# Attention on Trainium2: context exponentials before local ones, and the next tile's context scores before the last tile's values

## What is computed

```python
def context_attention(q, k, v):
    s = jnp.einsum('bqhd,bkhd->bhqk', q, k).astype(jnp.float32) * (HEAD_DIM ** -0.5)
    p = jax.nn.softmax(s, axis=-1).astype(v.dtype)
    return jnp.einsum('bhqk,bkhd->bqhd', p, v)
...
    s_loc = jnp.where(mask[None, None, :, None, :, :], s_loc, -jnp.inf)
    s_ctx = jnp.einsum('brnqhd,bphd->brnhqp', qb, k_ctx).astype(jnp.float32) * scale
    p = jax.nn.softmax(jnp.concatenate([s_loc, s_ctx], axis=-1), axis=-1).astype(v.dtype)
    o = (jnp.einsum('brnhql,brnlhd->brnqhd', p[..., :L], vg)
         + jnp.einsum('brnhqp,bphd->brnqhd', p[..., L:], v_ctx))
```

## Time and profile before

| | us |
|---|---|
| median of 3 runs | 2802.64 |
| lowest and highest | 2798.75, 2804.14 |
| the profiled execution | 2806.26 |
| its span, first to last instruction | 2804.5 |
| TensorE busy | 2680.5 (96%) |
| VectorE busy | 1698.7 (61%) |
| ScalarE busy | 1258.5 (45%) |

### The profile page before, as it was taken

How to read it: one execution, slowest core, us unless ns; L and a number is a source line. 1 busy time by engine, 2 the same in 40 slices (tenths; PEclk the granted TensorE clock), 3 DMA queues, 4 the chain that set the end, 5 groups by cost and what they waited for, 6 DMA issues and landing times.

```text
span 2804.5 us, 49219 instructions
## 1 busy us (share of the span) xinstructions
PE 2680.5 (96%) x21611; PEld 2008.6 (72%) x21611; DVE 1698.7 (61%) x2007; ACT 1258.5 (45%) x1795; POOL 192.3 (7%) x180
## 2 busy tenths in 40 slices
PE   6999999999999999959999999999999999999994
PEld 3555577666666698747877787778777877887783
DVE  3699234666323244466776767676766766676664
ACT  4000134555212132245656565555655555555554
POOL 0000001110000000010110111011101100110000
PEclk9999999999999999969999999999999999999997
DMA  8222222000333372267987988798888988898884
GB/s 258 90 90 75 60 56 50 14 1 24 90 90 90 90 218 106 98 213 249 290 281 267 298 278 282 264 299 279 280 279 285 294 265 282 281 297 262 283 278 167
DMA packets 457503, 543.73 MB, mean 194 GB/s; under 512 B 26304, under 2 KB 409387, under 8 KB 457290
## 3 DMA queue, kind: packets, MB, share of 16 engines
q1 hardware_dynamic: 449610, 519.60, 56.8%
q0 software_dynamic: 7680, 20.98, 3.4%
HBM read 513.27 MB, written 27.28 MB: 193 GB/s over the span
## 4 chain that ended last, share of the span: by engine, by line
PE 89%; DVE 5%; ACT 2%; SPq 2%; DMA 2%; issue 1%; POOL 0%; DVEq 0%; POOLq 0%; ACTq 0%
PE bank L651 84%; PE bank L654 5%; DVE arena L1643 2%; SPq L387 1%; ACT arena L1267 1%; DVE arena L1716 1%; ACT arena L1265 1%; DMA arena<-in_w_attn_o 0%; DVE arena L2044 0%; DVE arena L1726 0%; DMA arena<-in_w_in 0%; DMA arena<-in_cache_ctx_v 0%; DMA arena<-xhat,arena 0%; DVE arena L1723 0%; DMA yacc<-arena 0%
## 5 line engine op out<-in xcount | busy, mean ns | idle before, releaser
L651 PE MATMUL bank<-arena 128*64 128x128 f32 (+8 forms) x3716 | 735.6, 408 | 24.9 <-ACT arena L1267 10.6
L1974 DVE TENSOR_TENSOR slot_lo<-slot,e_hi 128x2048 fp32r<-128x2048 f32 x256 | 579.3, 2289 | 166.2 <-ACT e_hi L1456 162.5
L651 PEld LDWEIGHTS bank<-arena 128*128 128x128 f32 (+3 forms) x3716 | 431.9, 165 | 293.0 <-issue 216.8
L1456 ACT ACTIVATE e_hi<-slot 128x2048 fp32r<-128x2048 f32 x256 | 481.5, 1917 | 0.0
L651 PE MATMUL bank<-e_hi,xe_hi 128*128 128x512 f32 x1024 | 418.1, 408 | 0.0
L651 PE MATMUL bank<-e_hi,xe_lo 128*128 128x512 f32 x1024 | 404.7, 395 | 0.0
L651 PE MATMUL bank<-slot_lo,xe_hi 128*128 128x512 f32 x1024 | 400.3, 391 | 0.0
L651 PE MATMUL bank<-slot,arena 128*32 128x128 f32 (+1 forms) x10240 | 363.6, 297 | 6.1 <-DVE arena L1984 3.5
L651 PEld LDWEIGHTS bank<-slot,arena 128*32 128x32 f32 x10240 | 285.2, 111 | 72.6 <-issue 34.1
L1978 DVE TENSOR_TENSOR slot_lo<-slot,e_hi 128x2048 fp32r<-128x2048 f32 x128 | 288.8, 2288 | 77.9 <-ACT e_hi L1458 77.9
L654 PE MATMUL bank<-arena 128*128 128x128 f32 (+3 forms) x1415 | 207.0, 280 | 52.3 <-DVE arena L1572 12.8
(11 more groups left out here) (221 smaller groups left out, 2540.0 us busy)
## 6 DMA issues: line engine op xcount, KB each, us to landing
slot<-in_w_gate_e SPq DMA_DIRECT2D x128, 1024.0 KB, 5.7
slot<-in_w_up_e SPq DMA_DIRECT2D x128, 1024.0 KB, 9.1
slot<-in_w_down_e SPq DMA_DIRECT2D x128, 1024.0 KB, 6.9
arena<-in_w_in SPq DMA_DIRECT2D x68, 512.0 KB, 5.2
arena<-in_w_ada SPq DMA_DIRECT2D x48, 512.0 KB, 5.0
arena<-in_w_conv_pw SPq DMA_DIRECT2D x24, 256.0 KB, 5.7
arena<-in_w_attn_o SPq DMA_DIRECT2D x24, 256.0 KB, 5.4
yacc<-arena SPq DMA_DIRECT2D x10, 512.0 KB, 2.6
```

Source lines behind the costliest of these rows:

```text
L651: return nc.tensor.matmul(out, lhsT, rhs, start=start, stop=stop)
L1456: A_(halves(e_hi[c % 2])[:, :, rows4, :], halves(slot[q])[:, :, rows4, :], ACT.Copy).then_inc(ehi_ok, 1)
L1974: V_.tensor_tensor(halves(slot_lo[q])[:, :, rows4, :], halves(slot[q])[:, :, rows4, :], halves(e_hi[c % 2])[:, :, rows4, :].bitcast(F32), ...
```

## The change

- The exponentials of a tile stand as context A, context B, local A, local B. The semaphore `p_ok` is split: `pc_ok` counts context exponentials and `pl_ok` local ones.
- The groups of transposes stand as CA, CB, LA, LB, R in place of LA, CA, LB, CB, R. VectorE copies CA, LA and LB, ScalarE copies CB and R. CA and CB wait for `pc_ok`, the others for `pl_ok`.
- TensorE's round has `scores_context(g+1)`, which waits for `pc_ok`, ahead of `weigh(g-1)`.
- `weigh` takes the context parts first.
- The load of `vc` is issued ahead of the store of `state_v`.
- The load of the mask raises `bias_in`, and the mask's own semaphore goes.

VectorE's and GpSimd's work and order stay as they are, but for GpSimd's waits.

```diff
@@ -256,7 +256,7 @@
         w_d = A["w_down_e"][0].rearrange("e (k p) n -> e p k n", p=P)
 
 
-        rows_in, dwr_in, wr_in, mask_in = (sem(n) for n in ("rows_in", "dwr_in", "wr_in", "mask_in"))
+        rows_in, dwr_in, wr_in = (sem(n) for n in ("rows_in", "dwr_in", "wr_in"))
         x_in = [sem(f"x_in{tc}") for tc in range(3)]
         kraw_in, vc_in, fg_in = (sem(n) for n in ("kraw_in", "vc_in", "fg_in"))
         wo_in = [sem(f"wo_in{q}") for q in range(KD // 2)]
@@ -282,7 +282,7 @@
             sem(n) for n in ("ln_sum", "ln_mid", "ln_sq", "ln_var", "ln_std", "ln_norm", "ln_done"))
         bias_ok = sem("bias_ok")
         s_rem, s_loc, s_ctx, s_added = sem("s_rem"), sem("s_loc"), sem("s_ctx"), sem("s_added")
-        c_max, nmax_ok, p_ok = sem("c_max"), sem("nmax_ok"), sem("p_ok")
+        c_max, nmax_ok, pc_ok, pl_ok = sem("c_max"), sem("nmax_ok"), sem("pc_ok"), sem("pl_ok")
         tg_ready, tg_act, tg_dve, o_done = sem("tg_ready"), sem("tg_act"), sem("tg_dve"), sem("o_done")
         m_ready, m_sig, m_done = sem("m_ready"), sem("m_sig"), sem("m_done")
 
@@ -326,7 +326,7 @@
             nr = TILES[g % NTL][2]
             if nr == 0:
                 return [("P", True), ("R", False)]
-            return [("LA", True), ("CA", False), ("LB", True), ("CB", True), ("R", False)]
+            return [("CA", True), ("CB", False), ("LA", True), ("LB", True), ("R", False)]
 
         GROUPS = [(g, kind, by_dve) for g in range(NP) for kind, by_dve in groups(g)]
         GROUP_AT = {(g, kind): i for i, (g, kind, _) in enumerate(GROUPS)}
@@ -419,7 +419,7 @@
 
             sp.wait_ge(dw_ok, 1)
             sp.wait_ge(colv_ok, 1)
-            sp.dma_start(mask, A["window_masks"]).then_inc(mask_in, 16)
+            sp.dma_start(mask, A["window_masks"]).then_inc(bias_in, 16)
 
             def load_bias(hp):
 
@@ -439,8 +439,8 @@
             sp.wait_ge(ks_done, 2)
             sp.dma_start(O["state_k"][0, 0].rearrange("(t p) h d -> p t (h d)", p=P), kst).then_inc(state_out, 16)
             sp.wait_ge(v_done, 20)
+            sp.dma_start(vc, A["cache_ctx_v"][0, 0].rearrange("(t p) h d -> p t (h d)", p=P)).then_inc(vc_in, 16)
             sp.dma_start(O["state_v"][0, 0].rearrange("(t p) h d -> p t (h d)", p=P), vtok[:, 8:10, :]).then_inc(y_out, 16)
-            sp.dma_start(vc, A["cache_ctx_v"][0, 0].rearrange("(t p) h d -> p t (h d)", p=P)).then_inc(vc_in, 16)
             for hp in range(1, 4):
                 sp.wait_ge(b14_ok, 2 * hp)
                 load_bias(hp)
@@ -556,7 +556,6 @@
             nc.gpsimd.memset(glu, 0.0).then_inc(pads, 1)
 
             pool.wait_ge(conv_done, 1)
-            pool.wait_ge(mask_in, 16)
             def bias_rows(hp, h):
 
                 m = mask[:, 0:1, :].to_broadcast((P, SLOTS, GRID_W))
@@ -572,14 +571,16 @@
                     nc.gpsimd.tensor_tensor(b9[:, 1:9, :], b14[:, 2:10, :], mask[:, 1:9, :], ALU.add).then_inc(bias_ok, 1)
                     nc.gpsimd.tensor_tensor(b9[:, 0:1, :], b14[:, 10:11, :], mask[:, 9:10, :], ALU.add).then_inc(bias_ok, 1)
 
-            pool.wait_ge(bias_in, 64)
+            pool.wait_ge(bias_in, 64 + 16)
             for h in range(2):
                 bias_rows(0, h)
             for h in range(2):
                 bias_nine(0, h)
             for g in range(NP):
                 hp, i = divmod(g, NTL)
-                pool.wait_ge(p_ok, 2 * g + 2)
+                pool.wait_ge(pc_ok, 2 * g + 2)
+                if LOC[g]:
+                    pool.wait_ge(pl_ok, 2 * LOC0[g] + 2)
                 if g >= 2:
                     group_done(pool, g - 2, "R")
                 if LOC[g]:
@@ -590,7 +591,7 @@
                 nc.gpsimd.tensor_copy(rinv[:, g % 2, :].rearrange("p (a n) -> p a n", a=2),
                                       recip[:, g % 2, :].unsqueeze(2).to_broadcast((P, 2, DH))).then_inc(rinv_ok, 1)
                 if hp + 1 < HP and i == 1:
-                    pool.wait_ge(bias_in, 64 * hp + 128)
+                    pool.wait_ge(bias_in, 64 * hp + 128 + 16)
                     if hp == 0:
                         pool.wait_ge(ln_norm, 12)
                     else:
@@ -787,7 +788,7 @@
                 hp = g // NTL
                 qt, tok, nr, _ = TILES[g % NTL]
                 if g:
-                    pe.wait_ge(p_ok, 2 * g)
+                    pe.wait_ge(pc_ok, 2 * g)
                 for h in range(2):
                     keys = kcT[HALF[h], hp, :] if nr else kT[HALF[h], hp, TS:T]
                     last = mm(bank[3 + h][:, 0:PAST if nr else TP], qT[HALF[h], hp, P * qt:P * qt + P], keys, True, True)
@@ -798,7 +799,10 @@
                 nr = TILES[g % NTL][2]
                 for kind, _ in groups(g):
                     h = 1 if kind[1:] == "B" or kind == "P" else 0
-                    pe.wait_ge(p_ok, 2 * g + (2 if kind in ("R", "P") else h + 1))
+                    if kind in ("CA", "CB", "P"):
+                        pe.wait_ge(pc_ok, 2 * g + h + 1)
+                    else:
+                        pe.wait_ge(pl_ok, 2 * LOC0[g] + h + 1 if kind != "R" else 2 * LOC0[g + 1])
                     ring_free(pe, (g, kind))
                     out = ring_bank((g, kind))
                     if kind == "P":
@@ -827,7 +831,7 @@
                 ring_free(pe, (g, "O"))
                 out = ring_bank((g, "O"))
                 if nr:
-                    parts = [(b, vtok, tok // P + b) for b in range(4)] + [(4 + b, vc, b) for b in range(4)]
+                    parts = [(4 + b, vc, b) for b in range(4)] + [(b, vtok, tok // P + b) for b in range(4)]
                     if nr == 9:
                         parts.append((8, vtok, tok // P + 4))
                 else:
@@ -875,10 +879,10 @@
                     turn_weights(g - 1)
                 if g + 1 < NP and LOC[g + 1]:
                     scores_local(g + 1)
+                if g + 1 < NP:
+                    scores_context(g + 1)
                 if g:
                     weigh(g - 1)
-                if g + 1 < NP:
-                    scores_context(g + 1)
 
 
             pe.wait_ge(o_done, NP)
@@ -1261,10 +1265,12 @@
                 nr = TILES[g % NTL][2]
                 for h in range(2):
                     m = nmx[:, g % 2, h:h + 1]
-                    if nr:
-                        A_(Ploc[g % 2][h][:, 0:64 * nr], Ploc[g % 2][h][:, 0:64 * nr], ACT.Exp, bias=m, accum_out=sums[:, g % 2, h, 0:1])
                     n = PAST if nr else TP
-                    A_(Pctx[g % 2][h][:, 0:n], bank[3 + h][:, 0:n], ACT.Exp, bias=m, accum_out=sums[:, g % 2, h, 1:2]).then_inc(p_ok, 1)
+                    A_(Pctx[g % 2][h][:, 0:n], bank[3 + h][:, 0:n], ACT.Exp, bias=m, accum_out=sums[:, g % 2, h, 1:2]).then_inc(pc_ok, 1)
+                if nr:
+                    for h in range(2):
+                        m = nmx[:, g % 2, h:h + 1]
+                        A_(Ploc[g % 2][h][:, 0:64 * nr], Ploc[g % 2][h][:, 0:64 * nr], ACT.Exp, bias=m, accum_out=sums[:, g % 2, h, 0:1]).then_inc(pl_ok, 1)
 
             def leave_ring(g, kind):
 
```

## The result

The changed kernel takes 2810.93 us (median of 6 runs, 2809.98 to 2815.51), beside 2801.32 us for the kernel before in the same comparison (6 runs, 2798.75 to 2804.14): a ratio of 1.003, with a 95% interval of 1.0019 to 1.0041. It is slower, by about 9.6 us, and 2810.6 was predicted. The profiled execution took 2809.98 us, with a span of 2808.2.

The account below looks back on a forecast made before the run. TensorE was taken to bound rounds 3 to 6, with waits for exponentials at head pairs' ends. The terms 8.3 - 1.7 + 2.4 - 0.4 - 0.6 = +8.0 us, set on the median 2802.64, gave 2810.6 us, range 2803 to 2817.

Parts of the forecast that it names:

- boundary: First round of a head pair in the attention: 6.95 us against 7.96, 6.57 and 8.01, if at full clock.
- The loop: Attention rounds: weighing now stands in a loop through three engines, 6.95 us with 8 rows, 7.17 with 9.
- Rounds 2 to 10 and the first ones: Attention rounds: +2.1 us three times and +2.0 for the last head pair, together +8.3; first rounds -1.7.
- The -0.6: Wait for the last context exponentials at the attention's end: 3.06 us in the new order against 3.65.
- The clock: Half-clock stretches from TensorE idling in rounds 7 and 10: two of 1.2 us, +2.4, between none and 8.4.
- The -1.7: Three first rounds after a head pair's end: 6.95 us against 7.96, 6.57 and 8.01, all at full clock.
- The load of the cached values: Transfer issued ahead of the state's and wanted after the context scores: -0.4 us, between 0 and -0.48.
- What would show it: Signs in the profile after, among them later maximum starts, given round times and a stage of 258 us for 249.8.
- A wait for a context exponential in every round: Sign in the profile: the weight load of the context scores shows this wait in every round.
- The wait of round 10: TensorE's wait for context exponentials at a head pair's end: shrinks from 2.85 us to about 1.9.
- the gap decides: Rival: TensorE stays the bound with one 0.2 us gap less in 20 rounds; about -2, 2801 us; chance 0.13.
- the intended one: Rival: maximum runs straight after its scores, waits at head pairs' ends go; about -15, 2788 us; chance 0.07.

Follow-up runs that it names:

- e7: e1 with the reciprocal at the head of VectorE's iteration: 2788.40 us, ratio 0.9941.
- e1: Changed kernel with VectorE's queue reordered: both context maxima and the negated maximum ahead of the product of the tile before the last: 2795.24 us, ratio 0.9971.
- e4: Changed kernel with VectorE's product computed twice, the first time into an unused buffer: 2821.63 us, ratio 1.0069.
- e5: Kernel before with VectorE's product computed twice, the first time into an unused buffer: 2803.05 us, ratio 0.9995.
- e9: Changed kernel with the load of the cached values back behind the store of the states: 2811.42 us, ratio 1.0032.
- e6: Kernel before with only the load of the cached values moved ahead of the store of the states: 2804.08 us, ratio 1.0000.
- e3: Kernel before with only TensorE's context scores moved ahead of the values: 2865.89 us, ratio 1.0225.
- e2: Changed kernel with TensorE's order as before, values and then the next context scores: 2796.08 us, ratio 0.9977.
- e11: e7 with TensorE's old order, values ahead of the next context scores: 2815.22 us, ratio 1.0047.

## Why the prediction was right, and where it was not

Measured rounds in us, from the weight loads, beside the prediction's:

| round | before | predicted | after | e7 |
|---|---|---|---|---|
| boundary | 6.57 (7.96, 8.01) | 6.95 | 6.94 | 7.39 |
| 2, 8 rows | 6.57 | 6.95 | 6.94 | 6.35 |
| 3 to 6, mean | 7.08 | 7.17 | 7.16 | 6.68 |
| 7 | 5.77 | 6.53 | 6.52 | 5.65 |
| 8 | 5.09 | 5.60 | 5.56 | 5.22 |
| 9 and 10 | 10.27 | 10.37 | 10.32 | 8.05 |

- **The loop.** The maximum starts 0.40 us after the round's start (469.55 to 469.95), as summed; the negated maximum 1.90 later (1.92). Every round is within 0.05 us. That the path runs through the product is shown by e1 and e4, and that it did not before by e5.
- **Rounds 2 to 10 and the first ones.** From the second round's start to the last turn the profiles give 239.31 (457.61 to 696.92) and 245.53 (455.44 to 700.97), +6.22. Predicted, with no half clock: 8.3 - 1.7 - 0.6 = +6.0. The parts agree less well than the sum: rounds 2 to 10 grew by 7.9 us, the three boundaries changed by -1.7, and the last wait for exponentials changed by +0.02, not by -0.6. From the last round's start to the last turn it is 3.01 us before (693.91 to 696.92) and 3.03 after (697.94 to 700.97). The -0.6 is a slip: it takes off 0.64 us of context scores that are already in the 5.09 us of the old round 8, as 0.64 is in the 5.60 of the new one. An excess of 0.4 in the rounds and this 0.6 cancel, which is luck.
- **The clock, the term that was off in size.** Two stretches of 1.2 us were added; the profile after has none inside the attention, and e9, with the same rounds, one of 1.4. The term was +2.4 and measured 0 and 1.4 in two executions. The -1.7 is of the same kind: it rests on two stretches that the one profiled execution of before had. In the profiles of e5 and e6, whose rounds are those of the kernel before, the boundaries' rounds were 6.56, 7.71, 6.57 and 8.02, 6.57, 7.92.
- **From profile to median.** The profiled pair differs by 3.7 us of span: the attention begins 1.84 earlier (450.16 to 448.32), its first round is 0.33 shorter, rounds 2 to 40 are 6.22 longer, and what follows is 0.35 shorter. The earlier beginning isn't the change: the other runs' profiles, of either order, begin the attention at 448.35 to 449.63. The medians differ by 9.6, and by 8.5 in e9's comparison. The prediction's +8.0 is close to both, but partly by luck: without the clock it would have been +5.6. If a typical execution of before has fewer half-clock stretches than its profile, the two numbers meet (6.22 + 2.8 = 9.0). The clocks on record point that way: the profiled execution of before, at a mean granted clock of 0.981, is 4.9 us above its median, and that of after, at 0.984, is 1.0 below its own, where four of the six executions have 0.981 or 0.982. That makes up the 5.9 us between 3.7 and 9.6. In which stage the clock fell in the executions without a profile isn't shown, so how much of it belongs to the attention stays open.
- **The load of the cached values** was put at -0.4; the first round is 0.33 shorter (e6: 0.46). As e5 has 7.10 us with the late load, most of this is the wait of one execution, and no median shows it.
- **What would show it.** "A wait for a context exponential in every round" was too strong: rounds 5 and 6 show one (0.88 us at 480.70 and 487.87), rounds 3 and 4 none by name, since TensorE comes only 0.1 us early there. The wait of round 10 is 2.32 us before the weight load, not about 1.9. The margin between this forecast and "the gap decides" was as thin as the text had it. The stage was to take 258 us; it takes 255.2 in the profile, short mainly by the clock's term.
- **The rival "the intended one"** was worked out at 2788 us, if the maximum ran straight behind its scores. e7, which makes it do so, takes 2788.40. The sum of parts was another, though: it had the gain at the ends of head pairs alone, and e7 has on average 7.08 - 6.68 = 0.40 us of it in each of rounds 3 to 6, and loses 0.8 at each boundary. In the prediction the gap where the tile's shape changes was worth 0.2 a round only while TensorE is the bound. In e1, where it is in rounds 2 to 4, round 2 takes 6.35 us for 6.57, rounds 3 and 4 6.79 for 7.10, and rounds 5 and 6 6.56 and 6.57 for 7.10 and 6.99. Not all of that is the tile's shape: in the old order the nine-row rounds also wait for ScalarE's copy of the remainder, about 0.1 us in rounds 3 and 4 (the 36 loads of the weighing take 2.04 us for 1.95 in the changed kernel), and 0.34 and 0.23 us before the loads at 484.06 and 491.06 in rounds 5 and 6. The Trainium skill (TensorEngine Tiling (Array Packing), Key Properties) has a change of tiling mode drain TensorE; round 2 agrees with it, at the 0.2 us that the prediction had.

## What to carry to other kernels

When one engine's work is reordered, reorder its consumers' queues in the same way. An engine that works in program order passes a wait on to everything behind it, so results should be taken in the order in which they are made, and either half of the pair alone can lose what both together gain. Before counting a moved step as a win, look at what stands ahead of its consumer on the consumer's own engine. Doubling one suspected instruction, in the kernel before and in the one after, tells whether it is on the path: +0.2 us a round here in one, nothing in the other.

## What the hardware showed that was not expected

- The half clock behind a wait is not the same from run to run. The same round 10, with the same 2.32 us wait before its weight load, ran at a granted clock of 1.00 in the changed kernel (5.64 us) and once at 0.77 in e9 (7.05 us; e9's other two took 5.64 and 5.63). Behind 2.73 us without a multiplication all four rounds 7 of e3 ran low (0.82 in the one shown). A sum should hold such a term as a range and not as a count.
- Two scores of 64 rows side by side run faster than apart. In e1 the local and the context scores and the weighing of an eight-row round take 4.46 us (459.11 to 463.57). With the weighing between the scores, in e2, the same three parts take 4.66 (458.73 to 463.39). With nine rows it is 4.68 in e1 and 4.87 in e11 (474.84 to 479.71), so 0.2 us again; e2's 4.97 (472.62 to 477.59) also holds the wait of about 0.1 for the remainder's copy. That the change of shape is the cause fits both pairs, but no run tested it apart from the order.
